# Retention's 64 joint weight tiles of a three-block network multiplied in pairs, with seven block products for eight

## What is computed

```
h = rmsnorm(x)                                  # 1024 x 1024
proj = h @ w_in                                 # columns of q, k, v, r_gate, g_a, g_b and of a convolution
qh, kh = rotary(q, cos, sin), rotary(k, cos, sin) * 256 ** -0.5      # 4 heads of 256
vh = v                                          # 4 heads of 512
o = retention_chunkwise(qh, kh, vh, log_gamma)  # chunks of 128 tokens:
  scores = (qc @ kc.T) * decay;  inner = scores @ vc
  cross = (qi @ R) * xi;  R = R * gamma_c + (ki * zeta).T @ vi
mu, var = mean(o), mean((o - mu) ** 2)          # over the 512 of a head
o = (o - mu) * rsqrt(var + 1e-5) * gain * silu(r_gate)
y_b = o @ w_ret_proj
m = sigmoid(g_a) * y_a + sigmoid(g_b) * y_b     # y_a: the convolution's branch
x = rmsnorm(x + m @ w_out)
```

## Time and profile before

| | us |
|---|---|
| median of three executions | 4265.32 |
| span of the profiled execution | 4261.5 |
| what lies around the span (difference of the two) | 3.8 |
| retention: from its first load of weights to the first load behind the barrier | 927.8 to 1819.7 |

### The profile page before, as it was taken

How to read it: one execution, slowest core, us unless ns; L and a number is a source line. 1 busy time by engine, 2 the same in 40 slices (tenths; PEclk the granted TensorE clock), 3 DMA queues, 4 the chain that set the end, 5 groups by cost and what they waited for, 6 DMA issues and landing times. The chain is left out here.

```text
span 4261.5 us, 64163 instructions
## 1 busy us (share of the span) xinstructions
...
## 2 busy tenths in 40 slices
...
DMA packets 114612, 361.21 MB, mean 85 GB/s; under 512 B 12916, under 2 KB 14596, under 8 KB 114248
## 3 DMA queue, kind: packets, MB, share of 16 engines
...
...
## 5 line engine op out<-in xcount | busy, mean ns | idle before, releaser
L409 POOL CAST b_w_hi<-b_w 128x1024 fp32r<-128x1024 f32 x233 | 266.8, 1145 | 2952.3 <-PE ps L505 2262.3
L505 PE MATMUL ps<-b_hi,b_w_hi 128*128 128x512 f32 x1872 | 751.3, 401 | 31.7 <-DVE b_w_lo L425 9.9
L505 PE MATMUL ps<-b_hi,b_w_lo 128*128 128x512 f32 x1872 | 731.9, 391 | 0.0
L505 PE MATMUL ps<-b_lo,b_w_hi 128*128 128x512 f32 x1872 | 731.9, 391 | 0.0
L411 POOL TENSOR_TENSOR b_w_lo<-b_w,b_w_hi 128x1024 fp32r<-128x1024 f32 x233 | 601.8, 2583 | 18.6
L505 PE MATMUL ps<-h_hT_hi,b_w_hi 128*128 128x512 f32 x1216 | 500.1, 411 | 16.6 <-ACTq L2648 5.6
L505 PE MATMUL ps<-h_hT_lo,b_w_hi 128*128 128x512 f32 x1216 | 477.3, 392 | 0.0
L505 PE MATMUL ps<-h_hT_hi,b_w_lo 128*128 128x512 f32 x1216 | 476.8, 392 | 0.0
L505 PEld LDWEIGHTS ps<-b_hi,b_w_hi 128*128 128x128 f32 x1872 | 353.5, 189 | 121.4 <-issue 45.0
L505 PEld LDWEIGHTS ps<-b_lo,b_w_hi 128*128 128x128 f32 x1872 | 353.8, 189 | 79.5 <-issue 8.4
L505 PEld LDWEIGHTS ps<-b_hi,b_w_lo 128*128 128x128 f32 x1872 | 353.3, 189 | 74.9
...
## 6 DMA issues: line engine op xcount, KB each, us to landing
...
```

What stands on the lines that cost most here:

```text
L409: pool.tensor_copy(hi, w).then_inc(self.rounded, 1)
L505: ins = pe.matmul(out[:, t], w, y, start=start, stop=stop)
```

## The change

**Products.** Two weight tiles are taken as a 2x2 matrix of blocks (A11 and A12 the halves of the inner dimension of the first tile, A21 and A22 of the second), and h as another (inner halves by token halves, "near" 0 to 511 and "far" 512 to 1023). Their product took 8 block products, 12 matmuls each, and now takes 7 (`SevenProducts`): A11, A12, S2, S3, S1, A22, S4 in that order, where S3 = A11 - A21, S2 = A22 - S3, S1 = A11 + S2 and S4 = A12 - S2 are sums of weights. The other factors are the blocks of h and sums of them, T1 to T4, formed once. Matmuls for the 64 tiles: 32 x 7 x 12 = 2688 for 3072.

**GpSimd** forms the four sums of each pair (128x512) and splits the seven factors (CAST and subtraction, 128x512 each) into a ring of four slots: factor n is split once TensorE has finished product n-4. Before, it split two tiles a pair.

**Results.** ScalarE copies four intermediate states of a bank to SBUF, and VectorE adds PSUM to them four times (three for the gates' pairs F0 and F1, in line), 128x512 each.

**Buffers.** The stage `norm_and_first_tile` is gone: retention scales xT in place by halves of the tokens, forms T1 to T4 and their splits on VectorE (2048 wide), and the lower halves of h on GpSimd ahead of the weights' splits. q, k, v, the output o and the squares lie in xT; `late` holds the rotary tables, then the keys and the state R, then the head's gate; `parts` holds the gates' pairs. So the rotary tables are loaded anew in each unit (1 MB), behind the stores of o, on SyncE's queue, which also carries the weights' loads. One quarter of h, which T1 displaces, is kept in DRAM and split again behind the last unit.

**Else.** The reciprocal of the root is an Ln and an Exp on ScalarE. A unit's pairs are Q, K, V01, V23, F0, F1, G01, G23; scores, chunks and variance stand between whole products now. Behind the last unit GpSimd splits the convolution's first two tiles as before.

```diff
...
+class SevenProducts:
...
+    PAIRS = 8
+    IN_TWO_BANKS = (4, 5)
+    SLOTS = 4
...
+    def order(self, p):
+        return ("A11", "A12", "S2", "S3", "S1") + (("S4", "A22") if p in self.IN_TWO_BANKS else ("A22", "S4"))
...
+    def load_next(self, sp, u, p):
+        nxt = 2 * p + 2
+        sp.wait_ge(self.cut, self.nth(u, p, "S3"))
+        self.load(sp, "A21", u, nxt)
+        sp.wait_ge(self.cut, self.nth(u, p, "S1"))
+        self.load(sp, "A11", u, nxt)
+        for name in ("A12", "A22") if p in self.IN_TWO_BANKS else ("A22", "A12"):
+            if name == "A12":
+                sp.wait_ge(self.summed, self.weight_sums(u, p, 4))
+            else:
+                sp.wait_ge(self.cut, self.nth(u, p, "A22"))
+            self.load(sp, name, u, nxt)
+
+    def slot(self, p, name):
+        s = (7 * p + self.order(p).index(name)) % self.SLOTS
...
+        def split(name, src):
+            hi, lo = self.slot(p, name)
+            wait_alone(pool, self.done, self.nth(u, p, name), self.passed)
+            pool.tensor_copy(hi, src).then_inc(self.rounded, 1)
+            pool.wait_ge(self.rounded, self.nth(u, p, name))
+            pool.tensor_tensor(lo, src, hi, ALU.subtract).then_inc(self.cut, 1)
+
+        arrived("A11")
+        split("A11", raw["A11"])
+        arrived("A12")
+        split("A12", raw["A12"])
+        arrived("A21")
+        pool.tensor_tensor(raw["A21"], raw["A11"], raw["A21"], ALU.subtract).then_inc(self.summed, 1)
+        arrived("A22")
+        pool.wait_ge(self.summed, self.weight_sums(u, p, 1))
+        pool.tensor_tensor(S2, raw["A22"], raw["A21"], ALU.subtract).then_inc(self.summed, 1)
+        wait_alone(pool, self.summed, self.weight_sums(u, p, 2), self.passed)
+        split("S2", S2)
+        split("S3", raw["A21"])
+        pool.tensor_tensor(raw["A11"], raw["A11"], S2, ALU.add).then_inc(self.summed, 1)
+        wait_alone(pool, self.summed, self.weight_sums(u, p, 3), self.passed)
+        split("S1", raw["A11"])
+        if p not in self.IN_TWO_BANKS:
+            split("A22", raw["A22"])
+        pool.tensor_tensor(S2, raw["A12"], S2, ALU.subtract).then_inc(self.summed, 1)
+        wait_alone(pool, self.summed, self.weight_sums(u, p, 4), self.passed)
+        split("S4", S2)
+        if p in self.IN_TWO_BANKS:
+            split("A22", raw["A22"])
...
+        for k in range(KD // 2):
+            m = slice(k * P, k * P + P)
+            y_hi, y_lo = self.y_hi[name][:, k, :], self.y_lo[name][:, k, :]
+            pe.matmul(bank, hi[:, m], y_hi, start=first and k == 0, stop=False, skip_group_check=True)
+            pe.matmul(bank, hi[:, m], y_lo, start=False, stop=False, skip_group_check=True)
+            ins = pe.matmul(bank, lo[:, m], y_hi, start=False, stop=k == KD // 2 - 1, skip_group_check=True)
+        ins.then_inc(self.done, 1)
...
+    def copy(self, act, u, p, n, bank, dst, func=ACT.Copy):
+
+        act.wait_ge(self.done, self.finished(u, p, ("A11", "S2", "S1", "S4")[n]))
+        act.activation(dst, bank, func).then_inc(self.copied, 1)
+
+    def add_11(self, dve, u, p, bank, dst):
+        wait_alone(dve, self.copied, self.copies(u, p, 1), self.passed)
+        dve.wait_ge(self.done, self.finished(u, p, "A12"))
+        dve.tensor_tensor(dst, bank, dst, ALU.add).then_inc(self.added, 1)
+
...
+            pairs.load_first(sp)
...
+            sp.wait_ge(S["normed"], 12)
+            parked = d["half_park"].rearrange("p (k t) -> p k t", t=H)
+            sp.dma_start(parked, x[:, 0:4, far]).then_inc(S["quarter_parked"], 16)
+            sp.wait_ge(S["h_cut"], 1)
+            sp.dma_start(flat(rope), d["c_rope"]).then_inc(S["rope_loaded"], 16)
+            with sp.Fori(0, units) as u:
+                for p in range(pairs.PAIRS):
+                    pairs.load_next(sp, u, p)
+                    if p == G01:
+                        sp.wait_ge(S["parts_stored"], u * 64 + 96)
+                        sp.dma_start(quarter, parked).then_inc(S["quarter_loaded"], 16)
+                at = [sp.snap(u * (NV * P) + j * P) for j in range(NV)]
+                sp.wait_ge(S["o_ready"], u + 1)
+                for j in range(NV):
+                    sp.dma_start(d["o_park"][bass.ds(at[j], P), :], o[:, j, :]).then_inc(S["o_stored"], 16)
+                sp.dma_start(flat(rope), d["c_rope"]).then_inc(S["rope_loaded"], 16)
...
+            def cut_low(first, src):
+                hi, lo = stream.y_hi[:, first:first + 4, near], stream.y_lo[:, first:first + 4, near]
+                for n in range(4):
+                    pool.wait_ge(S["h_rounded"], first + n + 1)
+                    pool.tensor_tensor(lo[:, n, :], src[:, n, :], hi[:, n, :], ALU.subtract).then_inc(S["low_cut"], 1)
+
+            pool.sem_inc(pairs.done, pairs.SLOTS)
+            for n in range(2):
+                cut_low(4 * n, inputs[n])
+            with pool.Fori(0, units) as u:
+                for p in range(pairs.PAIRS):
+                    pairs.cut_pair(pool, u, p)
...
+            def product(u, p, name):
+                which, first = {"A11": (0, True), "S2": (0, False), "S1": (0, False), "S4": (0, False), "A12": (1, True),
+                                "S3": (1, True), "A22": (1, False) if p in (F0, F1) else (2, True)}[name]
+                if name == "S2":
+                    pe.wait_ge(pairs.copied, pairs.copies(u, p, 1))
+                elif name == "S1":
+                    pe.wait_ge(pairs.copied, pairs.copies(u, p, 2))
+                elif name == "S4":
+                    pe.wait_ge(pairs.copied, pairs.copies(u, p, 3))
+                elif name == "S3":
+                    pe.wait_ge(pairs.added, pairs.sums(u, p, 1))
+                elif name == "A22" and p in (F0, F1):
+                    pe.wait_ge(pairs.added, pairs.sums(u, p, 2))
+                pairs.multiply(pe, u, p, name, bank(p, which), first)
...
+            pe.wait_ge(S["low_cut"], 4)
             with pe.Fori(0, units) as u:
...
+                product(u, Q, "A11")
+                pe.wait_ge(S["low_cut"], 8)
+                product(u, Q, "A12")
+                for n, name in enumerate(("S2", "S3", "S1", "A22", "S4")):
+                    wait_alone(pe, S["h_cut"], n + 1, S["passed"])
+                    product(u, Q, name)
+                for p in (K, V01):
+                    products(u, p, pairs.order(p))
+                products(u, V23, ("A11", "A12"))
...
+                products(u, G01, ("A11", "A12", "S2", "S3", "S1", "A22"))
+                wait_alone(pe, S["o_kept"], u * NCH + NCH, S["passed"])
...
+            stream.multiply(pe, pair(core, 2), 0, late_cut=S["quarter_cut"])
...
+                act.activation(att[:, :], A, ACT.Ln, bias=core.const(LN_EPS)).then_inc(S["logged"], 1)
+                act.wait_ge(S["logged"], u + 1)
+                act.activation(att[:, :], att[:, :], ACT.Exp, scale=-0.5).then_inc(S["rooted"], 1)
...
+            spread_tokens(dve, chunks(att[:, :]), core.ident[:, :], core.scales[:, 1, :]).then_inc(S["spread_ready"], 1)
+            dve.wait_ge(core.x_parked[0], 16 * KD)
+            dve.wait_ge(S["spread_done"], 1)
+            for m, (first, t) in enumerate(((0, near), (4, near), (0, far), (4, far))):
+                for n in range(4):
+                    e = first + n
+                    dve.scalar_tensor_tensor(x[:, e, t], x[:, e, t], core.gains[:, 1, e:e + 1], scale[:, t], ALU.mult, ALU.mult) \
+                        .then_inc(S["normed"], 1)
+            dve.wait_ge(S["normed"], 16)
+            dve.tensor_tensor(T3, inputs[3], inputs[2], ALU.subtract).then_inc(S["h_summed"], 1)
+            dve.wait_ge(S["h_summed"], 1)
+            dve.tensor_tensor(T2, T3, inputs[0], ALU.add).then_inc(S["h_summed"], 1)
+            dve.tensor_tensor(T1, inputs[2], inputs[0], ALU.subtract).then_inc(S["h_summed"], 1)
+            dve.wait_ge(S["h_summed"], 3)
+            dve.wait_ge(S["low_cut"], 8)
+            dve.tensor_tensor(T4, T4, T2, ALU.subtract).then_inc(S["h_summed"], 1)
+            dve.wait_ge(S["h_summed"], 4)
+            low(pairs.y_lo["S2"], T2, pairs.y_hi["S2"], 13)
+            low(pairs.y_lo["S3"], T3, pairs.y_hi["S3"], 14)
+            low(pairs.y_lo["S1"], T1, pairs.y_hi["S1"], 15)
+            low(pairs.y_lo["A22"], T4, pairs.y_hi["A22"], 16)
+            low(pairs.y_lo["S4"], inputs[3], pairs.y_hi["S4"], 12)
...
+                add_11(u, Q)
+                add_others(u, Q)
+                add_11(u, K)
+                wait_alone(dve, S["rope_loaded"], u * 16 + 16, S["passed"])
+                dve.wait_ge(pairs.added, pairs.sums(u, Q, 4))
+                rope_cross(0, q)
+                add_others(u, K)
+                rope_join(0, q)
+                add_11(u, V01)
+                wait_alone(dve, pairs.copied, pairs.copies(u, K, 4), S["passed"])
+                dve.wait_ge(pairs.added, pairs.sums(u, K, 4))
+                rope_cross(1, k)
+                add_others(u, V01)
+                rope_join(1, k)
...
```

(18 more changed lines are left out.)

384 lines of the change are left out of this document (278 added, 106 removed).

## The result

The changed kernel took **4272.25 us** (median of 13 runs, 4265.94 to 4275.97), the kernel before 4264.15 us (13 runs on the same chip, 4258.14 to 4269.47): a ratio of 1.0019, with a 95% interval of 1.0012 to 1.0027, 8.1 us or 0.2% slower. Forecast were 4275.4 us, with 0.47 on slower by over 0.2% and 0.28 on no change that can be told; the result lies at that bound. The profiled execution has a span of 4266.0 us, for 4261.5. It took 4267.85 us, 4.4 less than the changed kernel's median, so that the two profiles lie 4.5 us apart and the medians 8.1. (Execution and span of the same run lie 1.7 to 2.1 us apart wherever both are on record; the 3.8 us of the table before set a median against the span of another execution. It is the same in the sum before and after.)

A forecast was written before the change was run, and what follows sets the result against it. TensorE was taken as the bound, with GpSimd becoming a second one. Matmuls saved -87.1, start +29, first unit +8, later units +36.6, output chain +17.6, end +6: +10.1 us, 4275.4 us; own range 4262 to 4296, overall 4232 to 4303.

The forecast's parts named there:

- What bounds the kernel: Retention before the change: TensorE is the bound, busy 217 of 220 us a unit; the other engines have slack.
- (a): TensorE's row: 384 matmuls removed at 0.2267 us each, -87.1 us; a pair then costs TensorE 19.04 us.
- (b): GpSimd's work for a pair: CAST 0.60, subtraction 1.28, hand-offs 0.08 us; 19.2 us in all, making it a second bound.
- (c): GpSimd and VectorE: VectorE operations with two SBUF inputs are paid in full by GpSimd; those with a PSUM input are not.
- (d): Stage's start: GpSimd and VectorE alternate before the third product; first pair done at 980.6 for 954.16, +29 us.
- (e): First unit, K and V01: GpSimd needs 53.0 us against TensorE's 38.1, less about 7 of lead, +8 us.
- (f): Later units, G01 through the loop's end to V01: GpSimd falls 12.2 us short a stretch, three stretches, +36.6 us.
- (g): Chain to the output: G23's S2 and S3 wait for ScalarE's copy and VectorE's sum, 4.4 x 4 = +17.6 us.
- (h): Stage's end: output and stores after the last product take 17.0 us to the barrier for 11.05, +6 us.
- The sum: Whole kernel: matmuls saved against start, first unit, later units, output chain and end, +10.1 us, giving 4275.4 us.
- The sign: Forecast slower; wrong if GpSimd's pair is under 17.5 us, or PSUM additions leave GpSimd unhindered and stretches lose under 5.
- B: Rival: GpSimd keeps its lead, its operations at the cheap end (17.7 us a pair); 4241 us (4232 to 4258), chance 0.22.

The follow-up runs named there:

- no_sums: The changed kernel without GpSimd's four sums of weights a pair (products wrong, all matmuls kept): 4200.27 us, ratio 0.9849 to the kernel before.
- act_casts: The changed kernel with the weights' rounding (CAST) on ScalarE instead of GpSimd, except a unit's first four factors: 4226.54 us, ratio 0.9910 to the kernel before.
- rope_psum: The changed kernel with nine of VectorE's twelve turning operations a unit reading their second input from PSUM (q, k wrong): 4247.23 us, ratio 0.9956 to the kernel before.
- g23_order: The changed kernel with ScalarE's copy of G23's A11 bank and VectorE's addition for G23 moved earlier: 4270.35 us, ratio 1.0013 to the kernel before.

## Why the prediction was right, point by point

- **What bounds the kernel, and (a).** Right: units without GpSimd's sums last 196.9 us, so the 384 matmuls are worth their distance of 0.2267 us and 87 us in all. TensorE's pause of 2.5 us at the loop's end, which the sum took as unchanged, is not: it is 0.15 to 0.3 us in no_sums and act_casts; in the changed kernel TensorE waits 3.2 to 3.5 us for GpSimd at that place, which would cover it.
- **(b) GpSimd's operations.** Right within 2%. The hand-off behind a sum was 0.33 us, not 0.08, three times a pair: some 0.8 us a pair too little.
- **(c) Exclusion.** Right, shown by rope_psum, which leaves GpSimd's program as it is. The additions from PSUM stayed at 0.69 us beside GpSimd, as forecast.
- **(d) Start.** 975.36 - 954.16 + 2.7 = 24 us, for 29. The turns of GpSimd and VectorE are as described, one operation of GpSimd for one of VectorE; S2 was ready at 959.4, not 963.5.
- **(e) First unit.** K and V01 waited 975.36 to 1023.57 less 38.1 = 10 us, for 8.
- **(f) and (g) Later units.** 217.0 - 197.9 = 19.1 us a unit, for 16.6. In it (g) is 2.1, not 4.4: the copy of A11, forecast 1.0 us late, was in time, and the sum behind A12 was 2.1 us late for 3.4. (f) is 17.0, not 12.2. What (f) had too little: GpSimd stood 4.0 us at the loop's end, for 2.6 in the sum, its hand-offs, and by the forecast's own sum the 2.3 us that (g) was shorter. These make more than the 4.8 that were missing, so another part of (f) was too dear; which, no run shows. g23_order shows that (g) was worth nothing by itself.
- **(h) End.** 1832.77 - 1817.03 (the last product's end, 2.72 behind its start at 1814.31) = 15.7 us, for 17.0: +4.7 for +6.
- **The sum.** -87.1 + 24 + 10 + 3 x 19.1 + 2.8 + 4.7 = +11.7, where the stage is 13.1 longer (2.8 are the last unit's waits in G23, 2.11 and 0.67). In the first unit TensorE also waits 1.7 us for GpSimd ahead of V23's S2, behind the first transposes, which is in no term. The forecast had +10.1 for the stage.
- **The step that failed** is one that the sum took as unchanged: the rest of the program. It is 8.6 us shorter in the two profiles, so that 13.1 became 4.5 there and 8.1 in the medians. Two errors, +3 in the stage and -5 to -9 behind it, partly cancelled in the number, and so did others within the stage (start 5 too dear, later units 2.5 each too cheap). That the time lies 3 us from the forecast is in part luck; the mechanism is not.
- **The sign** hung on something the forecast did not price as uncertain: the loop's end of GpSimd, 2.6 us in the sum without a range, is 4 us or nothing by where its instructions lie, and that is 5 us a unit. Taken as nothing, the kernel is at 4254, inside B's range, with the forecast's mechanism unchanged.
